# Hybrid decoder layer: x fetched tile by tile on both queues with a norm for each tile, and the first weights and the parts of h reordered

## What is computed

```python
def rmsnorm(x, g):
    xf = x.astype(jnp.float32)
    y = xf * lax.rsqrt(jnp.mean(xf * xf, axis=-1, keepdims=True) + EPS)
    return (y * g.astype(jnp.float32)).astype(x.dtype)
...
h = rmsnorm(x, norm1[l])
z = h @ w_in[l]
(z_rx, z_ry, z_q, z_kc, ...) = split(z)
# mixer A: causal conv of z_rx, RG-LRU scan, gate gelu(z_ry), product with w_rg_out
# mixer B: sparse attention with compressed, selected and window branches, product with w_nsa_out
x = x + (mg[:, :, 0] * y_a + mg[:, :, 1] * y_b) @ w_o[l]
h2 = rmsnorm(x, norm2[l])
x = x + (silu(h2 @ w_gate[l]) * (h2 @ w_up[l])) @ w_down[l]
```

## Time and profile before

| | |
|---|---|
| median of three runs | 485.9 us (485.82 to 485.99) |
| profiled execution, its own time | 487.44 us |
| its span | 485.7 us |
| PE busy (matmul) | 478.0 us, 98% |
| PE weight loads busy | 412.7 us, 85% |
| DVE busy | 355.0 us, 73% |
| ACT busy | 279.8 us, 58% |
| POOL busy | 15.1 us, 3% |
| read from HBM | 83.22 MB, 173 GB/s over the span |

### The profile page before, as it was taken

One profiled execution on the slowest core, in us unless ns is written; L12 is line 12 of the kernel. 1 busy time (PEld: TensorE's weight loads), 2 busy tenths in 40 slices (PEclk: granted clock), 3 DMA queues, 4 the chain that ended last, 5 costly groups with the idle time before them and its releaser, 6 DMA issues.

```text
span 485.7 us, 7347 instructions
## 1 busy us (share of the span) xinstructions
PE 478.0 (98%) x2803; PEld 412.7 (85%) x2803; DVE 355.0 (73%) x630; ACT 279.8 (58%) x451; POOL 15.1 (3%) x25
## 2 busy tenths in 40 slices
PE   7999999999989999999999999999999999999997
PEld 7998998788979778877787888888888888888886
DVE  3999899789895887757763767787777777754332
ACT  4755986675765896566763335755555445453320
POOL 2000200220000000000000000000000000000000
PEclk9999999999998999999999999999999999999999
DMA  8745966424224245333344362564555445554402
GB/s 311 272 162 208 373 271 255 174 88 173 88 97 164 88 173 194 152 128 135 106 154 165 104 251 88 188 246 177 187 206 209 175 173 181 200 224 175 173 1 86
DMA packets 12833, 84.73 MB, mean 174 GB/s; under 512 B 1536, under 2 KB 1792, under 8 KB 3072
## 3 DMA queue, kind: packets, MB, share of 16 engines
q1 hardware_dynamic: 12096, 82.32, 46.8%
q0 software_dynamic: 272, 1.05, 0.6%
q10 hardware_dynamic: 432, 0.91, 0.5%
HBM read 83.22 MB, written 1.05 MB: 173 GB/s over the span
## 4 chain that ended last, share of the span: by engine, by line
PE 93%; DVE 4%; ACT 2%; issue 0%; POOL 0%; POOLq 0%; DVEq 0%
PE bank L1109 18%; PE bank L1111 18%; PE bank L1110 18%; PE bank L1147 16%; PE bank L1150 8%; PE bank L1283 2%; PE bank L1319 2%; PE bank L1240 2%; PE bank L1521 1%; PE bank L1292 1%; DVE w_lo L671 1%; PE bank L1326 1%; PE bank L1323 1%; PE bank L1367 1%; ACT pbuf L473 1%; PE bank L1302 1%
## 5 line engine op out<-in xcount | busy, mean ns | idle before, releaser
L671 DVE TENSOR_TENSOR w_lo<-raw,w_hi 128x2048 fp32r<-128x2048 f32 x71 | 162.5, 2289 | 49.8 <-ACT w_hi L369 49.4
L369 ACT ACTIVATE w_hi<-raw 128x2048 fp32r<-128x2048 f32 x72 | 138.0, 1917 | 48.7 <-PE bank L1111 46.2
L1147 PE MATMUL bank<-h_hl,w_hi 128*128 128x512 f32 x336 | 80.3, 391 | 0.0
L1147 PEld LDWEIGHTS bank<-h_hl,w_hi 128*128 128x128 f32 x336 | 61.7, 188 | 11.9
L1109 PE MATMUL bank<-w_hi,h_hl 128*128 128x512 f32 x160 | 63.6, 398 | 0.0
L1111 PE MATMUL bank<-w_hi,h_hl 128*128 128x512 f32 x160 | 62.5, 390 | 0.0
L1110 PE MATMUL bank<-w_lo,h_hl 128*128 128x512 f32 x160 | 62.4, 390 | 0.0
L1109 PE MATMUL bank<-w_hi,act 128*128 128x512 f32 x150 | 59.1, 394 | 0.0
L1111 PE MATMUL bank<-w_hi,act 128*128 128x512 f32 x150 | 58.5, 390 | 0.0
L1110 PE MATMUL bank<-w_lo,act 128*128 128x512 f32 x150 | 58.4, 390 | 0.0
L1150 PEld LDWEIGHTS bank<-h_hl,w_lo 128*128 128x128 f32 x336 | 43.1, 191 | 1.6
(11 more groups left out here) (244 smaller groups left out, 744.6 us busy)
## 6 DMA issues: line engine op xcount, KB each, us to landing
raw<-stream_dram SPq DMA_DIRECT2D x72, 1024.0 KB, 4.8
w<-stream_dram SPq DMA_DIRECT2D x4, 1024.0 KB, 8.6
raw<-stream_dram SPq DMA_DIRECT2D x2, 512.0 KB, 7.3
xs<-x_dram POOLq DMA_DIRECT2D x1, 1024.0 KB, 5.4
out_dram<-xs SPq DMA_DIRECT2D x3, 256.0 KB, 2.0
xs<-x_dram ACTq DMA_DIRECT2D x1, 512.0 KB, 5.1
xs<-x_dram SPq DMA_DIRECT2D x1, 512.0 KB, 4.8
scr<-small_dram ACTq DMA_DIRECT2D x1, 320.0 KB, 8.8
```

The lines of the kernel that those rows point to most:

```text
L369: sc.activation(w_hi[:, i % HL, :], raw[:, i % RAW, :], ACT.Copy).then_inc(hi_ready, 1)
L671: ve.tensor_tensor(w_lo[:, i % HL, :], raw[:, i % RAW, :], f(w_hi[:, i % HL, :]), ALU.subtract).then_inc(lo_ready, 1)
L1147: ins = pe.matmul(acc(u + mt)[:, :], w_hi[:, s, c:c + P], a_hl[:, k, :, :].rearrange("p x s -> p (x s)"), start=n == 0, stop=n == 2 * KC - ...
```

## The change

Four things are changed, all of them before the first slot's product is done.

1. Each tile of x is fetched by two transfers of 64 rows, one from SP's queue and one from ACT's, tile 0 ahead of tile 1 on both. Each tile has its own semaphore, waited for at 32.
2. The norm is made for each tile by itself. ACT squares tile 0 and then half the columns of tile 1; DVE squares the other half of tile 1, and adds the two sums in the mean of tile 1 (one added small instruction). POOL has two small powers in place of one. The second block of six filling transposes shrinks to two.
3. The first half of slot 0 is split in quarters of the slot's 2048 columns (512 columns each), on ACT and on DVE, and PE waits for the second quarter at k = 2.
4. ACT makes four chunks of h ahead of the second half of slot 0 and four behind it. DVE makes two chunks, the second quarter, two chunks, and goes on as before.

```diff
@@ SP @@
-            sp.dma_start(xs[:, 0, :], x[0:P, :]).then_inc(x_in, 16)
+            for t in range(T2):
+                sp.dma_start(xs[0:64, t, :], x[t * P:t * P + 64, :]).then_inc(x_in[t], 16)
@@ POOL @@
-            rsqrt(NORM_X)
+            for t in range(T2):
+                rsqrt(NORM_X, t, 1)
@@ ACT @@
-            sc.dma_start(xs[:, 1, :], x[P:2 * P, :]).then_inc(x1_in, 16)
+            for t in range(T2):
+                sc.dma_start(xs[64:128, t, :], x[t * P + 64:(t + 1) * P, :]).then_inc(x_in[t], 16)
...
-            sc.wait_ge(x_in, 16)
+            sc.wait_ge(x_in[0], 32)
             sc.activation(xsq, xs[:, 0, :], ACT.Square, accum_out=ss[:, NORM_X, 0:1]).then_inc(squares, 1)
+            sc.wait_ge(x_in[1], 32)
+            sc.activation(scr[:, 3584:4096], xs[:, 1, 512:1024], ACT.Square, accum_out=ss[:, NORM_X, 2:3]).then_inc(x1_square, 1)
             sc.wait_ge(first_half, 16)
-            sc.activation(w_hi[:, 0, 0:1024], raw[:, 0, 0:1024], ACT.Copy).then_inc(hi_half, 1)
-            sc.wait_ge(landed[0], 16)
-            sc.activation(w_hi[:, 0, 1024:2048], raw[:, 0, 1024:2048], ACT.Copy).then_inc(hi_ready, 1)
+            for e in range(2):
+                sc.activation(w_hi[:, 0, e * 512:(e + 1) * 512], raw[:, 0, e * 512:(e + 1) * 512], ACT.Copy).then_inc(hi_half, 1)
...
-            chunks_hi(MISC["xT"], 0, G1)
+            chunks_hi(MISC["xT"], 0, G1, 0, 4)
+            sc.wait_ge(landed[0], 16)
+            sc.activation(w_hi[:, 0, 1024:2048], raw[:, 0, 1024:2048], ACT.Copy).then_inc(hi_ready, 1)
+            chunks_hi(MISC["xT"], 0, G1, 4, KC)
             split_hi(1)
@@ DVE @@
-            ve.wait_ge(x1_in, 16)
-            ve.scalar_tensor_tensor(out=scr[:, 3072:4096], in0=xs[:, 1, :], scalar=1.0, in1=xs[:, 1, :], op0=ALU.mult,
+            ve.wait_ge(squares, 1)
+            ve.tensor_scalar(ms[:, NORM_X, 0:1], ss[:, NORM_X, 0:1], 1.0 / D, EPS, ALU.mult, ALU.add).then_inc(ms_ready, 1)
+            ve.wait_ge(x_in[1], 32)
+            ve.scalar_tensor_tensor(out=scr[:, 3072:3584], in0=xs[:, 1, 0:512], scalar=1.0, in1=xs[:, 1, 0:512], op0=ALU.mult,
                                     op1=ALU.mult, accum_out=ss[:, NORM_X, 1:2]).then_inc(dve_chain, 1)
             chain[0] += 1
-            ve.wait_ge(dve_chain, chain[0])
-            ve.wait_ge(squares, 1)
-            mean(NORM_X, 1.0 / D)
-            ve.wait_ge(rs_ready, rs_count(NORM_X))
-            ve.wait_ge(x_in, 16)
+            ve.wait_ge(x1_square, 1)
+            link(ve.tensor_scalar(ss[:, NORM_X, 3:4], ss[:, NORM_X, 2:3], 1.0 / D, EPS, ALU.mult, ALU.add))
+            ve.scalar_tensor_tensor(out=ms[:, NORM_X, 1:2], in0=ss[:, NORM_X, 1:2], scalar=1.0 / D, in1=ss[:, NORM_X, 3:4],
+                                    op0=ALU.mult, op1=ALU.add).then_inc(ms_ready, 1)
             for t in range(T2):
+                ve.wait_ge(rs_ready, rs_count(NORM_X, t))
+                ve.wait_ge(x_in[t], 32)
                 ve.tensor_scalar(xn[:, t, :], xs[:, t, :], rs[:, NORM_X, t:t + 1], None, ALU.mult).then_inc(xn_ready, 1)
-            ve.wait_ge(hi_half, 1)
-            ve.tensor_tensor(w_lo[:, 0, 0:1024], raw[:, 0, 0:1024], f(w_hi[:, 0, 0:1024]), ALU.subtract).then_inc(lo_half, 1)
+            def first_quarter(e):
+                ve.wait_ge(hi_half, e + 1)
+                ve.tensor_tensor(w_lo[:, 0, e * 512:(e + 1) * 512], raw[:, 0, e * 512:(e + 1) * 512],
+                                 f(w_hi[:, 0, e * 512:(e + 1) * 512]), ALU.subtract).then_inc(lo_half, 1)
+            first_quarter(0)
...
-            chunks_lo(MISC["xT"], 0, G1, 0, 4)
+            chunks_lo(MISC["xT"], 0, G1, 0, 2)
+            first_quarter(1)
+            chunks_lo(MISC["xT"], 0, G1, 2, 4)
             ve.wait_ge(hi_ready, 1)
@@ PE @@
-                    pe.wait_ge(lo_half, 2)
+                    pe.wait_ge(lo_half, 3)
...
-            pe.wait_ge(rs_ready, rs_count(NORM_X))
+            pe.wait_ge(rs_ready, rs_count(NORM_X, 0))
             keep_busy(6)
...
-            keep_busy(6)
+            keep_busy(2)
...
                 for k in range(KC):
+                    if k == KC // 4:
+                        pe.wait_ge(lo_half, 2)
                     if k == KC // 2:
                         slot_ready(0)
```

More of the change, by code:

```diff
@@ L205, in hybrid_layer @@
         landed = [sem(f"landed{i}") for i in range(RAW)]
-        x_in, x1_in, small_in, prm_in, x_again = sem("x_in"), sem("x1_in"), sem("small_in"), sem("prm_in"), sem("x_again")
+        x_in = [sem(f"x_in{t}") for t in range(T2)]
+        small_in, prm_in, x_again, x1_square = sem("small_in"), sem("prm_in"), sem("x_again"), sem("x1_square")
         hi_ready, lo_ready = sem("hi_ready"), sem("lo_ready")
@@ L260, in hybrid_layer @@
         NORM_SHAPE = [(P, 2), (P, 16), (P, 16), (P, 16), (64, 1), (P, 2)]
-        RS_BEFORE = [0, 1, 3, 5, 7, 8]
+        RS_BEFORE = [0, 2, 4, 6, 8, 9]
         def rs_count(n, t=0):
```

## The result

The changed kernel took 488.54 us (median of 8 runs, 486.97 to 488.81), the kernel before beside it 486.73 us (8 runs, 485.82 to 487.60): the ratio on record over all runs is 1.0031, interval 1.0017 to 1.0045 (the two medians alone give 1.0037). It is slower, and 488.54 lies above the forecast's range of 484.2 to 487.0.

What follows compares the result with a forecast made beforehand. PE was taken to bound the kernel, fed without a wait from its first product at 12.00 us; -0.75 us there and +0.46 us of stall at k = 4 gave -0.3, from 485.9 to 485.6 us, range 484.2 to 487.0.

Steps and rivals of the forecast that it cites:

- What bounds the kernel: Whole kernel: PE, fed without a wait from 12.00 to 142 us, so only the start can shrink.
- x in four transfers: Start, loads: tile 0 at 4.4 us instead of 5.68, tile 1 still 5.9, weights on time; some 0.45 us per added issue.
- transfers of 64 rows: Rival, start: x moves at half rate, everything behind it 2.5 us later, +1.1 us, 487.0; chance 0.13.
- Norm by tile: Start, norm: scaled tile 0 at 7.9 us and tile 1 at 8.7, instead of 8.86 and 9.57; 0.9 us gained.
- the forecast's middle: Whole kernel: forecast time 485.6 us, with PE's real transposes taken to begin at 8.7 us.
- Where the transposes begin: Start, PE: the 16 real transposes begin between 7.95 and 9.42 us, 8.7 taken, depending on the clock's rise.
- The formula for the fillers: Start, PE: with the clock rising at r, the 34 fillers end at 6.51 + 0.49 (r - 2.80) us.
- its upper end of 9.42: Start, PE: latest begin taken for the real transposes; with it the change gives +0.4 us, 486.3.
- Four chunks ahead: Start, ACT: chunk 0 of h begins at 10.03 us and the first product comes at 11.25, 0.75 us earlier.
- The second quarter between the chunks: Slot 0, DVE: the 0.60 us quarter between chunks 1 and 2 stalls PE 0.46 us at k = 4.
- The clock in the attention: Rival, attention: the clock's fall after PE's 2.1 us wait may not happen, -1.6 us more, 484.0; chance 0.11.
- the late-x case: Start: slow 64-row transfers bring the first half at 10.4 us and the first product at 12.65; 487.0, chance 0.13.

Runs made afterwards that it cites:

- e9: Kernel before with 18 filling transposes in PE's attention wait and ACT making four chunks of h ahead of slot 0's second half: median 485.71 us.
- e6: Changed kernel with whole-tile loads of x, both quarters' low parts ahead of DVE's chunks, and 18 filling transposes in PE's attention wait: median 485.73 us.
- e12: Changed kernel with x fetched in whole tiles as before, plus 18 filling transposes in PE's attention wait: median 485.80 us.
- e1: Changed kernel with x fetched in whole tiles as in the kernel before, all else kept: median 485.89 us, ratio 0.999.
- e4: Changed kernel with whole-tile loads of x and both quarters' low parts ahead of DVE's chunks: median 487.28 us, ratio 1.0.
- e7: Kernel before with only 18 filling transposes added in PE's attention wait: median 486.01 us, ratio 0.9984.
- e2: Kernel before with only its loads of x changed to four transfers of 64 rows: median 489.36 us, ratio 1.0064.
- e3: Changed kernel with x's four transfers cut as 128 rows by 512 columns instead of 64 rows: median 487.55 us, ratio 1.0001.
- e10: Changed kernel as it is, run again beside the kernel before to count clock falls: median 487.21 us, ratio 1.0022.
- e5: e3 with 18 filling transposes in PE's attention wait and the small weights moved to SP's queue behind slots 1 and 2: median 485.75 us.
- e8: Changed kernel with 18 filling transposes added in PE's attention wait: median 487.05 us, ratio 1.001 to the unfilled kernel before.
- e11: e5 with both quarters' low parts ahead of DVE's chunks and four fillers fewer at the start: median 485.20 us, ratio 0.9975.

## Why the prediction was wrong

**What bounds the kernel.** Right. Of the 1.0 us between the two spans, 0.94 arose before slot 1, and it stayed to the end.

**"x in four transfers": the step that failed.** It took tile 0 at 4.4, tile 1 at 5.9 and the first half at 7.86, since x's bytes move at 406 to 426 GB/s. They moved at 226 to 268, and the three came at 5.46, 7.71 and 9.03. The issue was taken too low as well: the second transfer on each queue was put at 0.45 us and took 1.06 us more on ACT's and 0.80 more on SP's. The rival "transfers of 64 rows" stated this mechanism, had a chance of 0.13, and priced it at +1.1, 487.0. Like against like it cost 1.0 to 1.1 and the lower group lies at 487.0. That the price came out so well is partly luck, since its path was off: I had the late weights hold chunk 0; they landed only 1.2 late, not 2.5, and it was the norm of tile 1 that held it. The rows gave no case against this rival beyond "16 engines with work in both queues", which is no argument, and the Trainium skill's sentence named beside it deserved more than 0.13.

**"Norm by tile."** Tile 1's half squares (0.63 and 0.69) and small instructions came as costed. The power of tile 1 did not: 1.02 in place of 0.71. The sum for it was also added wrongly: 5.9 + 0.65 + 0.4 + 0.71 is 7.66, not 7.95; the forecast's middle doesn't use it. The norm by tile made no difference to the good: e9 without it is as quick as e6 and e12 with it.

**"Where the transposes begin."** The formula for the fillers held, and the rise of the clock does vary, as the forecast assumed: the 34 fillers ended at 8.36 in the changed kernel's profile and at 9.58 in that of the kernel before. The Trainium skill (TensorE: Matmul & The Clock Gate, What's actually happening) says that this moment differs from run to run of one kernel, and the traces agree: in three profiles of the changed start the fillers ended at 8.36, 8.92 and 9.20. The start of the transposes was 9.30, 9.51 and 9.53 in profiles of the whole-tile kernels e1, e4 and e6 and 8.93 in e12's. The middle that I took, 8.7, was early by that, and the two latest lie above its upper end of 9.42. The changed kernel's fillers ended at 8.36, which was no use to it, as xn wasn't there.

**"Four chunks ahead": right in sign, too large.** -0.75 was forecast for the first product; e9 alone measured -0.3 in the whole time. Some 0.2 of the difference is the gap at k = 4, which this move opens by itself since ACT's second half is then late for DVE, and the forecast put that at nothing. The rest is the start of the transposes: in e9's profile it was 9.15 and not 8.7.

**"The second quarter between the chunks": right in size.** The gap at k = 4 was forecast at 0.46 with DVE as releaser and measured 0.43. But the quarter is only half of its cause: without it ACT's second half is next in line and 0.23 stays (e6).

**The clock in the attention.** The mechanism was in the rivals, 1.6 us, and e7 shows it. The forecast used it in one direction only, a fall that goes away. It had noticed that the profiled execution stood 1.54 above the three runs, and drew no range from it: half of before's own runs are 1.6 higher. The range's upper end, 487.0, was the late-x case without the fall. With it, it is 488.6, and that is where the median lay. (The lower end, 484.2, doesn't fit its own rival either, which says 484.0.) So two things made the range fail: x's rate was given too little, and the spread of the baseline was left out.

## What to carry to other kernels

Cut a load that must arrive in parts by columns or by whole tiles, not by halves of the partitions on two queues: the DMA engines look just as busy, and the GB/s column alone tells. Before a sum of tenths is made, look whether the kernel's own times stand in two groups; if a profile shows a fall of TensorE's clock behind a wait, fill that wait and compare in the steady state. A mean granted clock says only that there was a fall, not where: e2 had the same 0.996 from another place. And where several engines reach the first product together, take the one move that frees the last of them and measure it alone: here the swap on ACT was worth as much as all the parts together.

## What the runs showed of the hardware

- Four transfers of 64 rows by 4 KB, two on each queue at once, moved x at 226 to 268 GB/s; 128 rows by 2 KB, same queues and sizes, had tile 1 there 1.7 us sooner. Whole tiles, one on each queue, moved at 410 to 416.
- Issuing them was dearer as well: two of 64 rows held ACT's queue for 1.46 us (three quarters of a microsecond each) and SP's for 1.20, where one of 128 rows took 0.40 and two of 128 rows by 2 KB took 0.88 and 0.90.
- The granted clock fell to 0.50 behind a wait of PE of 2.1 us in about half of the runs of the kernel before, for 3.4 us at a price of 1.6, and in no run of the seven kernels with the wait filled (0.999 or 1.0 in each). In the profiles of e2, e3 and e10 the same wait stands without the fall. Behind a wait of 2.24 us at the start it fell in e2's.
- POOL's power on one column took 0.55 us alone and 1.02 beside DVE's scaling of tile 0. It began at 8.89, DVE's scaling ended at 9.49, and it was done 0.42 later, at 9.91; in e3, e5, e8, e10 and e11 DVE waited for it in the same way (0.44 or 0.45). Alone on two columns it took 0.71. The Trainium skill (SBUF — State Buffer, Who interferes with whom) says that a DVE `tensor_scalar` in a mode with two ports and a GpSimd instruction shut each other out for a whole instruction. The times fit it, but no run here took the overlap away, so it is a reading and not shown.
